# A memory projection whose high and low token parts stand side by side in one 512-column pass

## The chip, the cores and the metric

The kernel runs on one core of one Trainium2 chip, as one launch. The metric is the device time of that launch in microseconds: median 962.98 of 3 runs, 962.02 to 963.68. TensorE (PE in the profile) multiplies, VectorE (DVE) and ScalarE (ACT) do the elementwise work, GpSimd (POOL) helps with some of it, SyncE (SP) issues nearly all transfers.

## The reference

One decoder layer on 512 tokens of width 2048, all in float32. The residual is normed, projected once to the queries, keys, values and gates of three groups of heads (6 block-sparse, 6 forgetting, 4 that attend into 256 memory tokens), each group's output is multiplied by SiLU of its gate, and an output projection, a norm and the residual close it. The part that the change touches is the projection of the memory:

```python
def rms_norm(x, g):
    xf = x.astype(jnp.float32)
    y = xf * lax.rsqrt(jnp.mean(xf * xf, axis=-1, keepdims=True) + EPS)
    return (y * g.astype(jnp.float32)).astype(x.dtype)
...
mkv = jnp.einsum('bmd,de->bme', rms_norm(mem, g_mem[layer]), w_mem_kv[layer])   # (1, 256, 1024)
km, vm = jnp.split(mkv, 2, axis=-1)
out_m = memory_attention(split_heads(qm, N_HEADS_MEM), split_heads(km, N_HEADS_MEM),
                         split_heads(vm, N_HEADS_MEM))
```

## The kernel before, in words

**High and low parts.** Every float32 matrix is split into a rounded high part (type F32R, fp32r in the profile) and the rest, the low part. A product is three passes of TensorE into one PSUM bank: high weight by high token, low weight by high token, high weight by low token. The helper `three` (lines 414 to 418) issues them, one line for each pass, and TensorE loads a 128x128 weight tile before each.

**Strips and pieces.** Weights are taken in strips of 128 output columns. A strip has 16 steps over the inner dimension and comes in two pieces of 8 steps. A piece is loaded by SP into `raw` (four slots); ScalarE writes its high part into `ring` (line 697, `hi`); VectorE (`lo`, `minus`, line 937) or GpSimd (`lo`, line 1279) writes its low part. Which of the two does the first 16 pieces is a list, `POOL_PIECES`: GpSimd has 0 to 5, 7 to 11, 13 and 15; VectorE has 6, 12 and 14. From then on VectorE does all.

**The memory projection.** The first 8 strips (t = 0 to 7) are `w_mem_kv` times the 256 memory tokens: t = 0 to 3 make the keys of the four memory heads, t = 4 to 7 their values. The tokens lie transposed in `memT`, indexed by half (high, low), step and token, with 256 columns for each half and step; so each pass has 256 columns and a bank of 512 is half used. They are multiplied by the gain of the norm but not yet by its reciprocal root. That root, spread over the partitions in `rstd_mem`, comes in where the strip leaves PSUM: line 1125 writes `k_mem`, `copy_v` (line 1012) writes `vT`. Strips alternate between two banks (`strip_ps`), and `strip_free` counts the evictions.

**The order around it.** The order of each engine is written out by hand. For each t, VectorE does: the eviction of key strip t - 1 (for t = 1 to 4), the norm factors and the scaling of one tile of x (`scale_tile`, lines 952 to 969; for t = 1 to 4), the low part of the key (line 937, `y<-k_mem,y`), from t = 5 the eviction of value strip t - 1, the low parts of the next strip's pieces where they are its own, and the low parts of transposed tiles of x (line 977). ScalarE does: the high part of the next strip's first piece, the high part of the key (line 833), the high part of the second piece, squares, and high parts of transposed tiles. So within one t, GpSimd can start on the second piece only when the key of strip t - 1 has been evicted by VectorE and copied by ScalarE. TensorE turns tiles of x between the two halves of strips 3 to 6 (line 454), and turns an evicted value strip back after the next strip (`turn_v`, line 464). Behind the eighth strip come 32 passes for the forget gate (line 575), and then the long run of strips of `w_in` over 512 tokens.

Of the kernel before, what the change touches and what calls it, by code (L numbers as in the profile page):

```python
# [29 lines left out]
F32 = mybir.dt.float32  # L30
F32R = mybir.dt.float32r
BF16 = mybir.dt.bfloat16
ALU = mybir.AluOpType
# [3 lines left out]
P = 128  # L37
D = 2048
S = 512
KT = D // P  # L40
QB = S // P
NMEM = 256
MB = NMEM // P
DH = 128
NA, NB, NM = 6, 6, 4
# [80 lines left out]
def build(nc, x, mem, w_in, b_forget, w_mem_kv, w_out, g_pre, g_post, g_mem, rel_bias, buckets, out):  # L126
    ctx = ExitStack()
    with ctx:
# [3 lines left out]
        def place(name, shape, dt, at=None):  # L132
            off = base[0] if at is None else at
            t = nc.alloc_sbuf_tensor_at(name, shape, dt, offset=off)
            if at is None:
                base[0] = off + (4 * int(np.prod(shape[1:])) + 31) // 32 * 32
            return t, off

        xT, _ = place("xT", [P, 2, KT, S], F32R)
        y, y_at = place("y", [P, 2, NH, S], F32R)  # L140
        raw, _ = place("raw", [P, RING, PW], F32)
# [8 lines left out]
        vT, vT_at = place("vT", [P, S], F32)  # L150
        ident, _ = place("ident", [P, P], F32)
        mask, _ = place("mask", [P, P], F32)
        bias_low, _ = place("bias_low", [P, 6 * P], F32)
        eps, _ = place("eps", [P, 1], F32)
        gains, _ = place("gains", [P, 2, KT], F32)
        relT, _ = place("relT", [BUCKETS + 1, NA], F32)
# [18 lines left out]
        ones, _ = place("ones", [P, P], F32, at=vT_at + 4 * P)  # L175
        gain_rows, _ = place("gain_rows", [KT, 2, P], F32, at=vT_at + 4 * 2 * P)
        k_mem, _ = place("k_mem", [P, NMEM], F32, at=vT_at + 4 * 2 * P)


        hot, _ = place("hot", [BUCKETS + 1, TABLE], F32, at=y_at + 4 * NAB * S)  # L180
# [31 lines left out]
        def sem(name):  # L212
            return ctx.enter_context(nc.semaphore(name))
# [30 lines left out]
        mem_squared = sem("mem_squared")  # L244
        diag_ready = sem("diag_ready")
        rstd_spread = sem("rstd_spread")
        k_taken = sem("k_taken")
        lo_pool = sem("lo_pool")
        part_done = sem("part_done")
# [163 lines left out]
        def _(pe):  # L413
            def three(dst, lhs, rhs, start, stop):

                pe.matmul(dst, lhs[0], rhs[0], start=start, stop=False, skip_group_check=True)  # L416
                pe.matmul(dst, lhs[1], rhs[0], start=False, stop=False, skip_group_check=True)  # L417
                return pe.matmul(dst, lhs[0], rhs[1], start=False, stop=stop, skip_group_check=True)  # L418

            def strip(t, par, rhs, n, between=None):  # L420

                if not isinstance(t, int) or t >= 2:
                    pe.wait_ge(strip_free, t - 1)
                for half in range(2):
                    by_pool, count = lo_count(2 * t + half)
                    pe.wait_ge(lo_pool if by_pool else lo_done, count)
                    w = ring[:, 2 * par + half].rearrange("p h (k m) -> p h k m", m=P)
                    for k in range(PIECE_KT):
                        kt = PIECE_KT * half + k
                        last = three(strip_ps[par][:, 0:n], (w[:, 0, k], w[:, 1, k]), (rhs[:, 0, kt], rhs[:, 1, kt]),  # L430
                                     kt == 0, kt == KT - 1)
                    last.then_inc(piece_used, 1)
                    if half == 0 and between is not None:
                        between()
# [22 lines left out]

            def turn_v(head_v, strip_v, blocks):

                pe.wait_ge(strip_free, strip_v + 1)  # L460
                if not isinstance(head_v, int) or head_v > 0:
                    pe.wait_ge(v_ready, head_v)
                for b in range(blocks):
                    last = pe.transpose(vt_ps[:, P * b:P * (b + 1)], vT[:, P * b:P * (b + 1)], ident[:])  # L464
                last.then_inc(v_turned, 1)
# [224 lines left out]
        def _(act):  # L690
# [137 lines left out]
            for t in range(STRIPS_MEM):  # L828
                next_strip = (t + 1, (t + 1) % 2, (t + 1) // 2)
                hi_strip(next_strip, 0)  # L830
                if 1 <= t <= NM:
                    act.wait_ge(strip_free, t)
                    act.activation(kmv[:, 4 * (t - 1)], k_mem[:], ACTF.Copy
                                   ).then_inc(k_hi, 1)
                hi_strip(next_strip, 1)
                if t == 0:
                    for half in range(2):
                        act.wait_ge(mem_landed[0][half], 16)
                    squares(0)
                    act.wait_ge(mem_squared, 1)  # L840
                    root(1, 0, MB)
                if t >= 6:
                    hi_v(t - 6, kmv[:, 4 * (t - 6) + 2], NMEM)
                if t in TURN_DURING:
                    pair, half = TURN_DURING[t]
                    hi_tiles(pair, 4 * half, 4 * half + 4)
                if t in SQUARE_DURING:
                    squares(SQUARE_DURING[t])
                    root(SQUARE_DURING[t], SQUARE_DURING[t])
                if t == 5:  # L850
                    act.wait_ge(forget_landed, 32)
                    act.wait_ge(wf_cleared, 1)
                    act.activation(wf[:, 0:KT * 64].rearrange("p (k c) -> p k c", c=64)[:, :, 0:NB], wf_raw[:],
                                   ACTF.Copy).then_inc(wf_hi, 1)
# [71 lines left out]
        def _(dve):  # L926
# [77 lines left out]
            def lo_k(head):  # L1004
                dve.wait_ge(k_hi, NM + head.a + 1)
                minus(kv[:, S:2 * S], strip_ps[1][:], kv[:, 0:S]).then_inc(strip_free, 1)

            def copy_v(strip_v, par):

                dve.wait_ge(piece_used, 2 * strip_v + 2)  # L1010
                if isinstance(strip_v, int) and strip_v < STRIPS_MEM:
                    dve.tensor_tensor(vT[:, 0:NMEM], strip_ps[par][:, 0:NMEM], rstd_mem[:], ALU.mult
                                      ).then_inc(strip_free, 1)
                else:
                    dve.tensor_copy(vT[:], strip_ps[par][:]).then_inc(strip_free, 1)

# [99 lines left out]
            for t in range(STRIPS_MEM):  # L1116
                if t == 1:
                    dve.wait_ge(rstd_spread, 1)

                    chain(dve.tensor_copy(rstd_mem[:], o_ps[:, 0:NMEM]))  # L1120
                if 1 <= t <= NM:
                    dve.wait_ge(piece_used, 2 * t)
                    if t > 1:
                        dve.wait_ge(k_taken, t - 1)
                    dve.tensor_tensor(k_mem[:], strip_ps[(t - 1) % 2][:, 0:NMEM], rstd_mem[:], ALU.mult
                                      ).then_inc(strip_free, 1)
                if t in SCALE_DURING:
                    scale_tile(SCALE_DURING[t])
                if 1 <= t <= NM:
                    dve.wait_ge(k_hi, t)  # L1130
                    minus(kmv[:, 4 * (t - 1) + 1], k_mem[:], kmv[:, 4 * (t - 1)]).then_inc(k_taken, 1)
                if t > NM:
                    if t > NM + 1:
                        dve.wait_ge(v_turned, t - 1 - NM)
                    copy_v(t - 1, (t - 1) % 2)
                for half in range(2):
                    lo_strip((t + 1, (t + 1) % 2, (t + 1) // 2), half)
                if t == STRIPS_MEM // 2 + 1:
                    for i, (bank, lo_, hi_) in enumerate(table_banks):
                        dve.wait_ge(table_made, i + 1)  # L1140
                        dve.tensor_copy(table[:, lo_:hi_], bank[0:NA, 0:hi_ - lo_]).then_inc(table_copied, 1)
                if t >= 6:
                    lo_v(t - 6, kmv[:, 4 * (t - 6) + 3], kmv[:, 4 * (t - 6) + 2], NMEM)
                if t == 0:
                    for half in range(2):
                        dve.wait_ge(mem_landed[1][half], 16)
                    dve.tensor_tensor_reduce(waste_mem[:], stage[:, 1], stage[:, 1], 1.0, 0.0, ALU.mult, ALU.add,
                                             sq[:, 1:2]).then_inc(mem_squared, 1)
                    dve.wait_ge(mem_squared, 1)
                    dve.wait_ge(squares_done, 1)  # L1150
                    rstd(1, 0, n=MB)
                    for i in range(MB):
                        dve.tensor_scalar(rstd_diag[:, i], ident[:], stat[:, 4, i:i + 1], None, ALU.mult
                                          ).then_inc(diag_ready, 1)
                if t in TURN_DURING:
                    lo_tiles(*TURN_DURING[t])
                if t == 5:
                    dve.memset(wf[:].bitcast(F32), 0.0).then_inc(wf_cleared, 1)
                    dve.wait_ge(wf_hi, 1)
                    wf_v = wf[:, 0:KT * 64].rearrange("p (k c) -> p k c", c=64)  # L1160
                    minus(wf_v[:, :, 32:32 + NB], wf_raw[:], wf_v[:, :, 0:NB]).then_inc(wf_ready, 1)
# [182 lines left out]
```

## Time and profile before

| what | value |
|---|---|
| median of 3 runs | 962.98 us (962.02 to 963.68) |
| profiled execution, first to last instruction (its span) | 961.3 us |
| median less span | 1.7 us |
| TensorE busy | 940.1 us, 98% of the span, 4556 passes |
| VectorE, ScalarE, GpSimd busy | 405.0, 312.0 and 93.1 us |
| mean granted clock of TensorE | 0.994 of full speed |
| the 384 passes of the memory projection, lines 416 to 418, 128x256 | 38.4, 37.2 and 37.2 us |

The profiled execution's own time has no figure apart from its span; the 1.7 us between span and median stand for launch and end around it. A group's busy time is the time from the start to the modelled end of its instructions; passes of TensorE overlap, so what one of them costs is the distance from its start to the start of the next. Idle time of an engine is put down to the instruction that released it.

### The profile page before, as it was taken

The numbers are of one execution on the slowest core, as the hardware profiler recorded it, in microseconds if no ns is written. First come the engines' busy times: TensorE is split into PE (matmuls) and PEld (weight loads), VectorE is DVE, ScalarE is ACT, GpSimd is POOL, SyncE is SP. The second block draws the span as 40 slices with busy tenths as digits, with TensorE's granted clock in tenths as the row PEclk, the third lists the DMA queues.
The fourth block names the chain that finished last, engine by engine and source line by source line (L and its number), as shares of the span: only waits on it lengthen the run. The fifth ranks groups of instructions, "written<-read, shape, count | busy, mean of one in ns | idle before, by whom it ended". The sixth has DMA issues, their size and how long they took to land.

```text
span 961.3 us, 12115 instructions
## 1 busy us (share of the span) xinstructions
PE 940.1 (98%) x4556; PEld 790.4 (82%) x4556; DVE 405.0 (42%) x724; ACT 312.0 (32%) x546; POOL 93.1 (10%) x84
## 2 busy tenths in 40 slices
PE   7799999999999999999999999999999999999996
PEld 5798888888888888888888888888888888888885
DVE  5884365444333333334343434343434254241424
ACT  6572333323232222223232323232323243242411
POOL 5542057000000000000010101010101000000000
PEclk9899999999999999999999999999999999999999
DMA  9934333343333333333333333333333127341216
GB/s 309 263 93 125 94 114 85 90 105 93 86 97 87 89 97 87 98 87 99 87 98 88 98 87 98 87 98 87 95 80 95 58 88 289 105 125 50 87 36 227
DMA packets 150943, 104.86 MB, mean 109 GB/s; under 512 B 5561, under 2 KB 136665, under 8 KB 149766
## 3 DMA queue, kind: packets, MB, share of 16 engines
q1 hardware_dynamic: 150630, 103.48, 38.5%
q10 hardware_dynamic: 288, 1.05, 0.3%
q8 instruction: 16, 0.26, 0.1%
q14 instruction: 9, 0.07, 0.0%
HBM read 100.29 MB, written 5.79 MB: 110 GB/s over the span
## 4 chain that ended last, share of the span: by engine, by line
PE 95%; DVE 2%; ACT 1%; DMA 1%; issue 0%; SPq 0%; DVEq 0%; ACTq 0%
PE strip_ps L416 25%; PE strip_ps L418 25%; PE strip_ps L417 25%; PE score_ps L416 3%; PE score_ps L418 3%; PE score_ps L417 3%; PE o_ps L520 3%; PE pt_ps L501 2%; PE score_ps L481 1%; PE score_ps L480 1%; PE score_ps L482 1%; PE o_ps L575 1%; PE vt_ps L464 1%; DMA stage<-in_mem_dram 1%; ACT y L736 1%; DVE y L937 1%
## 5 line engine op out<-in xcount | busy, mean ns | idle before, releaser
L416 PE MATMUL strip_ps<-xT,ring 128*128 128x512 f32 x896 | 352.0, 393 | 0.0
L418 PE MATMUL strip_ps<-xT,ring 128*128 128x512 f32 x896 | 349.3, 390 | 0.0
L417 PE MATMUL strip_ps<-xT,ring 128*128 128x512 f32 x896 | 348.9, 389 | 0.0
L418 PEld LDWEIGHTS strip_ps<-xT,ring 128*128 128x128 f32 x896 | 168.2, 188 | 35.6
L417 PEld LDWEIGHTS strip_ps<-xT,ring 128*128 128x128 f32 x896 | 168.4, 188 | 33.4
L416 PEld LDWEIGHTS strip_ps<-xT,ring 128*128 128x128 f32 x896 | 168.2, 188 | 33.3
L697 ACT ACTIVATE ring<-raw 128x1024 fp32r<-128x1024 f32 x128 | 135.1, 1058 | 34.3 <-PE strip_ps L418 34.3
L937 DVE TENSOR_TENSOR ring<-raw,ring 128x1024 fp32r<-128x1024 f32 x115 | 141.0, 1226 | 6.4 <-ACT ring L697 6.3
L1041 DVE MEMSET pace<- 128x1 f32 x36 | 2.1, 59 | 138.8 <-PE score_ps L482 138.8
L1313 POOL TENSOR_TENSOR bias<-bias,mask 128x128 f32<-128x128 f32 x6 | 6.6, 1097 | 553.0 <-DMA bias<-negc_dram 553.0
L937 DVE TENSOR_TENSOR xT<-raw,xT 128x1024 fp32r<-128x1024 f32 x32 | 39.0, 1224 | 41.9 <-ACT xT L697 41.6
L1001 DVE SCALAR_TENSOR_TENSOR q<-strip_ps,q 128x512 fp32r<-128x512 f32 x16 | 11.1, 692 | 102.6 <-ACT q L753 102.6
L753 ACT ACTIVATE q<-strip_ps 128x512 fp32r<-128x512 f32 x16 | 9.6, 598 | 127.9 <-PE strip_ps L418 127.9
L416 PE MATMUL strip_ps<-xT,y 128*128 128x512 f32 x128 | 50.0, 391 | 0.0
L418 PE MATMUL strip_ps<-xT,y 128*128 128x512 f32 x128 | 49.8, 389 | 0.0
L417 PE MATMUL strip_ps<-xT,y 128*128 128x512 f32 x128 | 49.8, 389 | 0.0
L416 PE MATMUL score_ps<-xT,y 128*128 128x512 f32 x128 | 49.8, 389 | 0.0
L417 PE MATMUL score_ps<-xT,y 128*128 128x512 f32 x128 | 49.8, 389 | 0.0
L418 PE MATMUL score_ps<-xT,y 128*128 128x512 f32 x128 | 49.8, 389 | 0.0
L775 ACT ACTIVATE prob<-prob,negmax 128x128 f32<-128x128 f32 (+3 forms) x48 | 27.0, 563 | 67.1 <-DVE negmax L1046 66.7
L697 ACT ACTIVATE xT<-raw 128x1024 fp32r<-128x1024 f32 x32 | 33.7, 1059 | 43.9 <-PE score_ps L418 33.1
L416 PE MATMUL strip_ps<-y,ring 128*128 128x256 f32 x128 | 38.4, 300 | 6.2 <-DVE ring L937 3.3
(164 smaller groups left out, 1021.9 us busy)
## 6 DMA issues: line engine op xcount, KB each, us to landing
raw<-in_w_in_dram SPq DMA_DIRECT2D x112, 512.0 KB, 4.1
raw<-in_w_out_dram SPq DMA_DIRECT2D x32, 512.0 KB, 4.0
raw<-in_w_mem_kv_dram SPq DMA_DIRECT2D x16, 512.0 KB, 6.2
stage<-in_x_dram SPq DMA_DIRECT2D x4, 1024.0 KB, 7.6
xres<-in_x_dram SPq DMA_DIRECT2D x4, 1024.0 KB, 7.5
out_dram<-o_sb SPq DMA_DIRECT2D x16, 256.0 KB, 3.5
toep_dram<-table_dram SPq DMA_DIRECT2D x1, 1536.0 KB
bias<-toep_dram SPq DMA_DIRECT2D x6, 256.0 KB, 2.6
```

The costliest lines, as they stand in the source:

```text
L416: pe.matmul(dst, lhs[0], rhs[0], start=start, stop=False, skip_group_check=True)
L417: pe.matmul(dst, lhs[1], rhs[0], start=False, stop=False, skip_group_check=True)
L418: return pe.matmul(dst, lhs[0], rhs[1], start=False, stop=stop, skip_group_check=True)
L464: last = pe.transpose(vt_ps[:, P * b:P * (b + 1)], vT[:, P * b:P * (b + 1)], ident[:])
L480: pe.matmul(dst[:, 0:n], qs[0], kv[:, 0:n], start=True, stop=False, skip_group_check=True)
L481: pe.matmul(dst[:, 0:n], qs[1], kv[:, 0:n], start=False, stop=False, skip_group_check=True)
L501: last = pe.transpose(pt_ps[g % 2][:, P * i:P * (i + 1)], src, ident[:])
L520: last = pe.matmul(o_ps[:, first:S], v, pT[:, hl_p, kb, first:S], start=(hl_v, hl_p, kb) == (0, 0, 0), stop=(hl_p == 1 and kb == nb - 1), ...
L697: act.activation(dst[:, 0], raw[:, slot], ACTF.Copy).then_inc(hi_done, 1)
L775: last = act.activation(prob[:, i % 2, 0:n], prob[:, i % 2, 0:n], ACTF.Exp, scale=-1.0, bias=negmax[:, i:i + 1], accum_out=rowsum[:, i:i + 1])
L937: return dve.tensor_tensor(dst, a_, hi_.bitcast(F32), ALU.subtract)
L1001: dve.scalar_tensor_tensor(out=q[:, 1], in0=strip_ps[0][:], scalar=SCALE, in1=q[:, 0].bitcast(F32), op0=ALU.mult, op1=ALU.subtract).then_i ...
```

## The change

It is made at four places. In `strip`, where the tokens are the memory's (n is 256), one pass of 512 columns takes the high weight over the high and the low tokens side by side, `rhs[:, :, kt]`; its results stand in the two halves of the bank. A second pass of 256 columns puts low weight by high token on the right half. So a step has two passes in place of three, of 768 columns together as before. In the evictions, `scale_halves` multiplies both halves by `rstd_mem` into `halves` (one instruction of 512 elements, over the place of `bias_low`, which is first written much later) and then waits for itself; a second instruction adds the halves. `strip_free` now counts the multiplication. ScalarE's copy of the key and TensorE's turn of the value wait for two new semaphores that count the addition.

```diff
@@ build
-        bias_low, _ = place("bias_low", [P, 6 * P], F32)
+        bias_low, bias_low_at = place("bias_low", [P, 6 * P], F32)
...
+        halves, _ = place("halves", [P, 2, NMEM], F32, at=bias_low_at)
...
+        k_scaled = sem("k_scaled")
+        v_scaled = sem("v_scaled")
@@ strip (TensorE)
                         kt = PIECE_KT * half + k
+                        if n == NMEM:
+
+                            pe.matmul(strip_ps[par][:, 0:2 * n], w[:, 0, k], rhs[:, :, kt], start=kt == 0, stop=False,
+                                      skip_group_check=True)
+                            last = pe.matmul(strip_ps[par][:, n:2 * n], w[:, 1, k], rhs[:, 0, kt], start=False,
+                                             stop=kt == KT - 1, skip_group_check=True)
+                            continue
                         last = three(strip_ps[par][:, 0:n], (w[:, 0, k], w[:, 1, k]), (rhs[:, 0, kt], rhs[:, 1, kt]),
                                      kt == 0, kt == KT - 1)
@@ turn_v (TensorE)
-                pe.wait_ge(strip_free, strip_v + 1)
+                if isinstance(head_v, int) and head_v < NM:
+                    pe.wait_ge(v_scaled, head_v + 1)
+                else:
+                    pe.wait_ge(strip_free, strip_v + 1)
@@ the strips of the memory (ScalarE)
                 if 1 <= t <= NM:
-                    act.wait_ge(strip_free, t)
+                    act.wait_ge(k_scaled, t)
@@ (VectorE)
+            def scale_halves(t, par):
+
+                one_row = rstd_mem[:]
+                twice = bass.AP(one_row.tensor, one_row.offset, [one_row.ap[0], [0, 2], [1, NMEM]])
+                dve.tensor_tensor(halves[:], strip_ps[par][:].rearrange("p (h t) -> p h t", h=2), twice, ALU.mult
+                                  ).then_inc(strip_free, 1)
+                dve.wait_ge(strip_free, t + 1)
+
             def copy_v(strip_v, par):
 
                 dve.wait_ge(piece_used, 2 * strip_v + 2)
                 if isinstance(strip_v, int) and strip_v < STRIPS_MEM:
-                    dve.tensor_tensor(vT[:, 0:NMEM], strip_ps[par][:, 0:NMEM], rstd_mem[:], ALU.mult
-                                      ).then_inc(strip_free, 1)
+                    scale_halves(strip_v, par)
+                    dve.tensor_tensor(vT[:, 0:NMEM], halves[:, 0], halves[:, 1], ALU.add).then_inc(v_scaled, 1)
...
-                    dve.tensor_tensor(k_mem[:], strip_ps[(t - 1) % 2][:, 0:NMEM], rstd_mem[:], ALU.mult
-                                      ).then_inc(strip_free, 1)
+                    scale_halves(t - 1, (t - 1) % 2)
+                    dve.tensor_tensor(k_mem[:], halves[:, 0], halves[:, 1], ALU.add).then_inc(k_scaled, 1)
```

## Rows read from the trace of the kernel before

**Rows 1.** The page, busy time by engine: us (share of the span) xinstructions.

```profile
PE 940.1 (98%) x4556; PEld 790.4 (82%) x4556; DVE 405.0 (42%) x724; ACT 312.0 (32%) x546; POOL 93.1 (10%) x84
```

**Rows 2.** What TensorE waited for, 0 to 200 us: in total, times, longest.

```profile
PE strip_ps L416 <- DVE ring L937: 3.3, 1, 3.3
PE strip_ps L416 <- POOL ring L1279: 2.8, 3, 1.2
PE o_ps L549 <- DVE rstd_diag L1153: 2.5, 1, 2.5
```

**Rows 3.** The chain that ended last, 24 to 48 us: start, length, work.

```profile
28.14 0.43 DVE rstd_mem L1120
28.59 0.42 DVE k_mem L1125
...
31.11 2.56 DVE y L937
...
33.77 0.42 DVE k_mem L1125
...
36.28 2.50 DVE y L937
...
40.06 0.55 PE strip_ps L416
```

**Rows 4.** VectorE in order of time: start, length, line, operation, output<-inputs.

```profile
28.93 0.14 DVE L952 TENSOR_SCALAR stat<-sq 128x1 f32<-128x1 f32 x1
...
38.70 1.21 DVE L937 TENSOR_TENSOR ring<-raw,ring 128x1024 fp32r<-128x1024 f32 x1
39.84 0.41 DVE L1125 TENSOR_TENSOR k_mem<-strip_ps,rstd_mem 128x256 f32<-128x256 f32 x1
...
45.74 0.42 DVE L937 TENSOR_TENSOR y<-k_mem,y 128x256 fp32r<-128x256 f32 x1
...
59.41 0.42 DVE L1012 TENSOR_TENSOR vT<-strip_ps,rstd_mem 128x256 f32<-128x256 f32 x1
...
99.88 0.69 DVE L1001 SCALAR_TENSOR_TENSOR q<-strip_ps,q 128x512 fp32r<-128x512 f32 x1 [7.16 <-ACT q L753]
```

**Rows 5.** GpSimd in order of time, 30 to 45 us.

```profile
30.50 2.88 POOL L1279 TENSOR_TENSOR ring<-raw,ring 128x1024 fp32r<-128x1024 f32 x1 [4.09 <-ACT ring L697]
35.67 2.82 POOL L1279 TENSOR_TENSOR ring<-raw,ring 128x1024 fp32r<-128x1024 f32 x1 [2.30 <-ACT ring L697]
38.84 5.65 POOL L1279 TENSOR_TENSOR ring<-raw,ring 128x1024 fp32r<-128x1024 f32 x2 [0.34 <-ACT ring L697]
```

**Rows 6.** ScalarE in order of time, 29 to 39 us.

```profile
29.05 0.42 ACT L833 ACTIVATE y<-k_mem 128x256 fp32r<-128x256 f32 x1 [5.37 <-DVE k_mem L1125]
...
37.72 1.04 ACT L697 ACTIVATE ring<-raw 128x1024 fp32r<-128x1024 f32 x1
```

**Rows 7.** TensorE in order of time: passes of 256 and of 512 columns.

```profile
56.26 0.36 PE L416 MATMUL strip_ps<-y,ring 128*128 128x256 f32 x1
...
66.70 0.38 PE L464 MATMUL vt_ps<-ident,vT 128*128 128x128 f32 x2
...
78.96 0.28 PE L416 MATMUL strip_ps<-y,ring 128*128 128x256 f32 x1
...
80.04 0.28 PE L416 MATMUL strip_ps<-y,ring 128*128 128x256 f32 x1
...
300.27 0.39 PE L418 MATMUL strip_ps<-xT,ring 128*128 128x512 f32 x1
...
307.75 0.39 PE L418 MATMUL strip_ps<-xT,ring 128*128 128x512 f32 x1
```

**Rows 8.** Busy time by stretch: PE, PEld, DVE, ACT, POOL, granted clock, DMA share, GB/s.

```profile
24.00:39.30 15.30, 10.25 (x82) 9.79 (x80) 13.95 (x24) 9.01 (x12) 8.58 (x5) 1.00 0.93 274
39.40:46.10 6.70, 6.04 (x28) 6.07 (x29) 6.56 (x9) 1.36 (x2) 5.08 (x2) 0.50 0.84 229
46.20:48.00 1.80, 1.80 (x18) 1.80 (x17) 0.74 (x2) 1.62 (x5) 0.00 (x0) 1.00 1.20 295
```

## The prediction

> **What bounds the kernel now.** I read the page first. TensorE is busy for 940.1 of 961.3 us; VectorE, the next, for 405.0 [rows 1]. So a time changes only where TensorE's own passes change or where it stands idle. Next the list of what TensorE waited for. Up to 200 us it has three entries that bear on the memory projection: 3.3 us for a low part by VectorE, 2.8 us in three waits for low parts by GpSimd, 2.5 us for the norm factors [rows 2]. Asked for from 48 us on, the same view lists nothing. So from there every us that TensorE starts earlier or later, and every us that its passes take less, goes into the end one to one.
>
> The third view, the chain of waits around the longest gap, says who sets it. It runs on VectorE from 28.14 to 39.91 us (38.70 + 1.21): root copied, key strip 0 evicted, norm factors and scaling of a tile, low part of the key, key strip 1 evicted, the same again, and last the low part of piece 6, for which TensorE starts strip 3 at 40.06 [rows 3, 4]. The two evictions in that chain are the ones that the change makes longer. The fourth view, granted clock by stretch, shows a price of the gap: the clock is 1.00 up to 39.3 us, 0.50 from 39.4 to 46.1, and 1.00 again from 46.2 [rows 8]: the two levels, 2.4 and 1.2 GHz, with some 6.8 us at the lower one, 6.1 of them work. The gap of 2.5 us before the spreading of the norm factors [rows 2] lies in the stretch at 1.00 and lowered nothing.
>
> **What the passes save.** A step of the projection has three passes of 256 columns and gets one of 512 and one of 256. By the time from start to start, 9 passes of 256 take 80.04 - 78.96 = 1.08 us, 120 ns each [rows 7]. 33 passes of 512 (11 steps of 3 between the two rows) take 307.75 - 300.27 = 7.48 us, 227 ns each [rows 7]. So two narrow passes, 240 ns, become one wide pass of 227: 13 ns a step. What goes is a fixed cost of a pass and not columns. No row shows a wide pass over two separate runs of tokens. Its bounds: 0 ns saved, if it costs what its two halves cost apart; and 39 ns, if the step cost nothing beyond its 768 columns at 2.4 GHz (320 ns against 360). I take 13, since the 512-column row is the same kind of pass with the same type and the same load of weights.
>
> The saving counts only where TensorE does not wait afterwards. Strips 0 to 2 end in the waits above, so there it makes the gap wider and nothing else. The first half of strip 3 runs at half clock; I give it nothing (at most 8 steps, 0.1 us). The second half of strip 3 and strips 4 to 7 are 8 + 64 = 72 steps: 72 x 13 ns = 0.94 us saved (0 to 2.8).
>
> The Trainium skill speaks against this term: TensorE: Matmul & The Clock Gate, Back-to-back issue gap, gives N/2.4 + 2.5 ns between warm passes. By that rule, an estimate, a step would save one fixed cost of 2.5 ns, 0.18 us in all, and the change would come out 0.8 us worse than by the rows. The trace does not agree with its fixed cost: 256 columns at 2.4 GHz are 107 ns and the row has 120.
>
> **What the evictions add.** The old one takes 0.42 us and the next VectorE instruction starts 0.34 us after it (28.59 to 28.93) [rows 3, 4]; ScalarE's copy of the key starts at 29.05, 0.46 us after it [rows 6]. The new one has two parts. The multiplication reads 512 elements from PSUM; the nearest row of that size takes 0.69 us [rows 4]. Waiting for itself costs little: the copy before the eviction ends at 28.57 and the eviction, which waits for it, starts at 28.59 [rows 3]. The addition reads 256 elements twice from SBUF; the same form on the key takes 0.42 us where GpSimd is idle [rows 4]. So the old 0.42 becomes 0.69 + 0.02 + 0.42 = 1.13, and both the next instruction of VectorE and ScalarE's copy come 0.71 us later. Bounds of that: 0.60 if the broadcast row comes free, and 0.42 + 2.5 more where GpSimd is in the way.
>
> GpSimd can be. The low part of the key, 256 elements that take 0.42 us alone, takes 2.56 and 2.50 us in the chain, and ends 0.3 and 0.3 us behind GpSimd's subtractions, which run from 30.50 to 33.38 and from 35.67 to 38.49 [rows 3, 5]. (The Trainium skill, SBUF — State Buffer, Who interferes with whom: an instruction of VectorE with two SBUF inputs and one of GpSimd that reads SBUF exclude each other, the first to start going first. The trace agrees.) The eviction itself reads PSUM and one SBUF tile and is not held up. The addition is of the other sort. For t = 1 it falls at 28.59 + 0.71 = 29.30; GpSimd is idle until 30.50, and its next piece waits for ScalarE, which waits for this key [rows 5, 6]. For t = 2 the eviction moves from 33.77 to 34.48, the addition to 35.2; GpSimd's piece ends by 33.38 + 0.71 = 34.1, and the next again waits for this key. So both additions are clear, by about 1 us. GpSimd, ScalarE and VectorE all move by the same 0.71 each time, and so does what they do to each other. **The chain of the gap grows by 2 x 0.71 = 1.42 us**, and strip 3 starts at 41.48 instead of 40.06.
>
> The other six evictions. For t = 3 the multiplication starts at 39.84 + 1.42 = 41.26, the addition at 41.97; there GpSimd has piece 8 until 38.84 + 1.42 + 2.83 = 43.1, so the addition ends near 43.4, over 1 us late [rows 4, 5]. Behind it stand ScalarE's copy, the high part and low part of piece 9, and VectorE's scaling and low key. Piece 9 is then done at about 47.7, and TensorE needs it for the second half of strip 4, at 56.26 before [rows 7]: hidden by 10 us. The slot of piece 9 also comes free some 3 us later for SP's load of piece 13, needed well behind that. t = 4 has no chain to TensorE that is close. The value strips: the first is evicted at 59.41 and turned by TensorE at 66.70 [rows 4, 7], 7 us for 0.7. The next strips' pieces (12, 14) lie behind these evictions on VectorE and are needed one strip later, each over 4 us off. `strip_free` comes 0.27 us later and guards a bank that TensorE wants one strip later. These cost nothing while the distances stand; gone, each would cost 0.71.
>
> **Sum.** +1.42 (gap) - 0.94 (72 steps) = +0.48 us against the profiled span of 961.3, so 961.8. The median of the runs lies 1.7 us above the span, which I carry over: 962.98 + 0.48 = **963.5**. This assumes that as much work falls into half clock as before. It has a small side: if all 6.8 us of half clock now met work, where 0.7 met the gap, +0.35, 963.8. With the bounds of the pass (0 to 2.8) the case itself runs from 961.6 to 964.8.
>
> **Rivals.**
> *The half clock ends when it ended.* If it returns near 46.15 whatever TensorE has done, strip 3's later start loses only half as much: 1.42 us of half-rate work is 0.71 of full-rate work. Then 0.71 - 0.94 = -0.23, 962.8. For it: no start or end of TensorE's work marks 46.15. Against: nothing in one trace separates this from a length that counts from the start.
>
> *The clock does not fall.* Piece 5 now comes 0.71 us later, at 34.1, and strip 2 can't start its second half before; its 8 steps of 0.347 us then end near 36.9, after a stop inside the strip, and the gap is some 4.5 us long. Before, 6.1 us of work (40.06 to 46.15) ran at half rate, 3.05 lost. If the new split of work and idle time escapes the lower level, 0.48 - 3.05 - 0.1 = -2.7, 960.3. For it: a 2.5 us gap escaped. Against: the large gap grows.
>
> *GpSimd gets in ahead of piece 6 (the other side).* VectorE begins piece 6 at 38.70 and GpSimd piece 8 at 38.84 [rows 4, 5]: 0.14 us decide. Both move by 1.42 by my sum; ScalarE's high part (37.72 + 1.04) sets GpSimd, and GpSimd's own piece 7 sets VectorE. If VectorE comes 0.15 us later against it, piece 6 waits for piece 8, 2.83 us, and strip 3 with it: 0.48 + 2.83 = +3.3, 966.3.
>
> *The wide pass costs its columns only* (39 ns a step): 1.42 - 2.8 = -1.4, 961.6. The row of 227 ns for 213 ns of columns speaks against it. That passes do not fall from 384 to 256 is not to be expected; the code is unconditional there.
>
> **How the numbers follow.** Forecast 0.40; half clock ends in its place 0.20; clock does not fall 0.13; GpSimd first 0.12; columns only 0.05; an addition or another stall that I placed wrongly, +1 to +3 us, 0.10, six of these ten past the line. A measurement of this kernel can tell 0.2%, 1.9 us, from no change. Faster: 0.13. Slower: 0.12 + 0.06 = 0.18. Same: 0.69. The range takes in all but the collision and the worst stalls: 960.2 to 965.5; the forecast's own is 961.6 to 964.8.
>
> **What would show it.** 128 passes fewer, 4428. Strips 4 to 7 with 347 ns a step. k_mem's first addition near 29.3 and 0.42 us long, the one at t = 3 over 1 us long. Strip 3 starting at 41.5 with the last wait for piece 6. The granted clock tells the first two rivals from the forecast, and the order of pieces 6 and 8 the third. A wait of TensorE behind 50 us, or additions of 2 us in the gap's chain, would make it wrong.

## The result, and the profile after

| | runs | median, us | range |
|---|---|---|---|
| before | 19 | 962.80 | 962.02 to 963.87 |
| the change | 19 | 964.26 | 962.98 to 966.16 |

The ratio is 1.0016, with a 95% interval of 1.0009 to 1.0023: slower by 1.5 us (0.16%), and less than the 0.2% that I took for the limit of what can be told. A second measurement, in another session, gave 1.0018 (1.0009 to 1.0027). Forecast was 963.5, "same" at 0.69. The forecast direction (+0.48) is right and its size a third of what came. The rest of this document is about the missing 1.0 us: what of it the runs explain, and what they leave open.

The page of the profiled execution: 128 passes fewer, TensorE no less busy, VectorE 7 us busier.

```profile
span 962.8 us, 11867 instructions
...
PE 940.5 (98%) x4428; PEld 783.9 (81%) x4428; DVE 411.8 (43%) x732; ACT 311.6 (32%) x546; POOL 94.4 (10%) x84
```

What TensorE waited for, up to 200 us, as [rows 2]. The wait for piece 6 grew from 3.3 to 4.2 us; nothing is listed behind it.

```profile
PE strip_ps L436 <- DVE ring L951: 4.2, 1, 4.2
PE strip_ps L436 <- POOL ring L1301: 2.7, 3, 1.3
PE o_ps L563 <- DVE rstd_diag L1175: 2.6, 1, 2.6
```

The chain around the gap, as [rows 3] (start, length, work).

```profile
29.53 0.44 DVE rstd_mem L1142
29.99 0.70 DVE halves L1026
30.71 0.42 DVE k_mem L1148
...
33.23 2.55 DVE y L951
...
35.88 0.70 DVE halves L1026
36.61 0.42 DVE k_mem L1148
...
39.12 2.49 DVE y L951
41.61 1.15 DVE ring L951
42.75 0.14 issue
42.89 0.77 PE strip_ps L436
```

The absolute times mislead here. This execution copied the root at 29.53 where the other did at 28.14 [rows 3]: the first load of memory tokens, which the change doesn't touch, was the start of both chains and took 7.38 us against 5.98. A second profile of the change copied it at 28.05. So read distances from the copy. From there to strip 3 it is 42.89 - 29.53 = 13.36 us; before, 40.06 - 28.14 = 11.92. That is +1.44, for two evictions of 0.70 + 0.03 + 0.42 in place of 0.42. At the other end, the 32 passes for the forget gate (line 575 before, 589 after) are a good end mark, because from their start to the end of the span it is 880.8 us in both kernels (961.3 - 80.54; 962.8 - 82.00):

```profile
81.87 0.38 PE L478 MATMUL vt_ps<-ident,vT 128*128 128x128 f32 x2
82.00 0.48 PE L589 MATMUL o_ps<-xT,wf 128*128 128x512 f32 x1
```

From the copy to that mark: before 80.54 - 28.14 = 52.40 us, after 52.47. By the two profiled executions, the change costs 0.1 us once the start is taken out. The medians say 1.5. One pair of profiles did not show what the change does on average.

The clock is the first hint (stretches as in [rows 8]):

```profile
30.00:41.00 11.00, 8.14 (x46) 6.64 (x44) 10.55 (x18) 8.41 (x12) 5.36 (x2) 1.00 0.89 314
41.10:47.80 6.70, 4.91 (x15) 4.27 (x16) 6.53 (x11) 1.86 (x3) 4.59 (x3) 0.50 0.65 175
47.90:60.00 12.10, 12.10 (x79) 10.07 (x78) 11.93 (x22) 10.02 (x22) 6.73 (x3) 1.00 0.31 87
```

Half clock lasted about as long as before (6.8 us), but began earlier against the work: strip 3 began at 42.89 and met 4.9 us of it, not 6.04 [rows 8]. By the start of strip 3 and the end of the half clock it is 5.0 against 6.1, and half of the difference, 0.56 us, was given back. So this pair went as my first rival said: +1.44 - 0.56 - 0.83 (the passes, below) = +0.05, where 0.07 was read.

VectorE, in order of time, at the key of strip 2 (t = 3). The addition is held until GpSimd is done, as forecast, at 1.88 us for 0.42:

```profile
41.53 1.21 DVE L951 TENSOR_TENSOR ring<-raw,ring 128x1024 fp32r<-128x1024 f32 x1
42.67 0.68 DVE L1026 TENSOR_TENSOR halves<-strip_ps,rstd_mem 128x512 f32<-128x512 f32 x1
43.38 1.88 DVE L1148 TENSOR_TENSOR k_mem<-halves 128x256 f32<-128x256 f32 x1
```

And GpSimd (start, length), which began piece 8 at 41.67, 0.14 us behind VectorE's piece 6, the same distance as in [rows 4, 5]:

```profile
41.67 3.30 POOL L1301 TENSOR_TENSOR ring<-raw,ring 128x1024 fp32r<-128x1024 f32 x1 [0.35 <-ACT ring L711]
```

### The profile page after: what moved, and what is told of

The parts are those of the page before. It is cut to its first block, busy times and chain, and to the rows that moved or that the text cites. A ratio compares the mean times of both kernels' runs of the same rounds, so it can differ in the third digit from the quotient of the medians.

```text
span 962.8 us, 11867 instructions
## 1 busy us (share of the span) xinstructions
PE 940.5 (98%) x4428; PEld 783.9 (81%) x4428; DVE 411.8 (43%) x732; ACT 311.6 (32%) x546; POOL 94.4 (10%) x84
## 4 chain that ended last, share of the span: by engine, by line
PE 95%; DVE 2%; ACT 1%; DMA 1%; issue 0%; SPq 0%; DVEq 0%; ACTq 0%
PE strip_ps L420 24%; PE strip_ps L422 24%; PE strip_ps L421 24%; PE score_ps L422 3%; PE score_ps L421 3%; PE score_ps L420 3%; PE o_ps L534 3%; PE strip_ps L436 2%; PE pt_ps L515 2%; PE strip_ps L438 1%; PE score_ps L495 1%; PE score_ps L494 1%; PE score_ps L496 1%; DMA stage<-in_mem_dram 1%; PE o_ps L589 1%; PE vt_ps L478 1%
## 5 line engine op out<-in xcount | busy, mean ns | idle before, releaser
L951 DVE TENSOR_TENSOR ring<-raw,ring 128x1024 fp32r<-128x1024 f32 x115 | 143.1, 1245 | 6.1 <-ACT ring L711 6.0
L436 PE MATMUL strip_ps<-y,ring 128*128 128x512 f32 x128 | 48.5, 418 | 7.0 <-DVE ring L951 4.2
```

Source lines behind the costliest of these rows:

```text
L436: pe.matmul(strip_ps[par][:, 0:2 * n], w[:, 0, k], rhs[:, :, kt], start=kt == 0, stop=False, skip_group_check=True)
L951: return dve.tensor_tensor(dst, a_, hi_.bitcast(F32), ALU.subtract)
```

## The experiments

Every kernel ran in 9 to 11 timed executions, beside 31 to 33 of the kernel before on the same chip in each of three sessions (medians of before: 962.37, 962.38, 962.46). "Mean clock" is the mean granted clock over all executions of a kernel; 0.001 of it is 1.9 us at half clock. Before has 0.9938, 0.9943 and 0.9939; the change has 0.9918 (19 executions, the first result) and 0.9925 (11, the second measurement, beside the 0.9943). It is a weak witness. All 14 profiles also show 3.6 to 6.6 us of half clock at the very end, where TensorE has no work left, and four of them (the change, evictions only, two strips old, before with 6 fillers) show 3.4 us between 8 and 14 us. So two executions can differ by 0.002 and more without any difference behind the gap.

The theories that the expectations name: **A**, my sum as it stands (passes -0.94, evictions +1.42, half clock alike). **B**, A and a longer gap that on average puts more work at half clock. **C**, the changed program delays the start of the memory stage. **D** came later: with the clock up, VectorE becomes the slower engine behind the gap.

### Each half of the change alone

**Passes only.** The new passes are put into the kernel before, with the old eviction.

```diff
+                        if n == NMEM:
+                            pe.matmul(strip_ps[par][:, 0:2 * n], w[:, 0, k], rhs[:, :, kt], start=kt == 0, stop=False, ...)
+                            last = pe.matmul(strip_ps[par][:, n:2 * n], w[:, 1, k], rhs[:, 0, kt], start=False, ...)
+                            continue
```

> The 512-column pass and the 256-column pass of the change, with the old eviction, which reads the left half of the bank only: the product of the low weights and the low tokens' part are left out of k and v. The chain of the gap is as before. Theory A (my sum: passes -0.94 us, evictions +1.42 us, half clock as before): 0.8 to 1.0 us faster than before, strip 3 starts as far behind the copy of the root as before (11.9 us). Theory B (A, and a longer gap puts more work into half clock on average): the same here, since the gap grows by only 0.1 to 0.2 us. Theory C (the passes or the changed program delay the start of the memory stage, 28.14 to 29.53 us in the two profiles): slower than before or no faster, with the root copied near 29.5 us in the profile.

Measured: 961.30 us, ratio 0.9990 (0.9981 to 0.9999), -1.1 us by the medians. From copy to strip 3 it is 40.32 - 28.40 = 11.92, exactly the old gap. Theories A and B stand. The new passes do not delay the copy of the root: it came at 28.40.

**Evictions only.** The old passes, with the two-part eviction on the left half twice.

```diff
-                dve.tensor_tensor(halves[:], strip_ps[par][:].rearrange("p (h t) -> p h t", h=2), twice, ALU.mult
+                left = strip_ps[par][:, 0:NMEM]
+                left2 = bass.AP(left.tensor, left.offset, [left.ap[0], [0, 2], [1, NMEM]])
+                dve.tensor_tensor(halves[:], left2, twice, ALU.mult
...
-                    dve.tensor_tensor(k_mem[:], halves[:, 0], halves[:, 1], ALU.add).then_inc(k_scaled, 1)
+                    dve.tensor_tensor(k_mem[:], halves[:, 0], halves[:, 1], ALU.max).then_inc(k_scaled, 1)
```

> The three old passes, with the two-part eviction: the multiplication reads the left half twice, and a maximum of the two equal halves stands in for the addition, so the result is whole. Theory A: +1.4 us against before, strip 3 starts 13.3 to 13.4 us behind the copy of the root. Theory B: +1.4 plus up to 1 us, since the gap is as long as that of the change less 0.1 us. Theory C: +1.4, or no more than A if the passes are the cause.

Measured: 964.75 us, 1.0025 (1.0015 to 1.0035), +2.4 us. The chain grew by what was forecast (42.97 - 29.59 = 13.38 from copy to strip 3, +1.46), so the evictions cost about 0.9 us more than the chain shows. The two halves add up to the whole (-1.1 + 2.4 = +1.3). The missing us is on the side of the evictions, and not in the passes. B had room for it, A had not. Two things in this run speak against taking that for a proof of B. The mean clock is 0.9932 beside 0.9938, so hardly lower. And its profile copied the root at 29.59, late like that of the change (29.53).

This leaves theory C open for the evictions. In the 14 profiles of this study the copy lies between 28.05 and 29.59. The six profiles of kernels with the two-part eviction in the chain show 28.05, 28.28, 28.54, 28.88, 29.53 and 29.59, the eight others 28.14 to 28.88. The evictions come behind the copy, and the change has it at 28.05 too, so nothing in the traces says that they move it. But no timed execution shows where its copy was, and a later one on average would go into the time in full.

### The gap filled with other passes

The fillers are passes into a bank that nobody reads then. They are meant to keep TensorE at work until piece 6 is ready; n is 10 for the change, 8 and later 6 for the kernel before.

```diff
                 strip(t, t % 2, memT, NMEM, lambda: between(t))
+                if t == 2:
+                    for _ in range(n):
+                        pe.matmul(o_ps[:, 0:NMEM], ones[:], rstd_diag[:], start=True, stop=True)
```

> The change, with 10 more passes (the form of line 549, 0.35 us each) in the gap before strip 3, into a bank that nobody reads then; they should end before piece 6 is ready. The granted clock should then stay at 1.00 up to strip 7. Against the change: 2.5 us faster (half of the 5.0 us that its profile shows at half clock) in executions like the profiled one. Against the kernel before: A, that loses 3.05 us to half clock: -2.6 us. B: the kernel before loses less than that on average, so -1.5 or less, and the change loses about 1 us more than it.

> The kernel before, with 8 of those passes in its gap. Clock at 1.00 throughout the memory stage. A: 3.0 us faster than before, and the change with its gap filled is +0.4 to +0.6 us against this one while the plain pair differs by +1.46, which then needs B. If the filled pair differs by 1.4 as well, the clock explains none of it and one of my two terms (1.42, 0.94) is wrong.

Measured: the change filled 962.88, 1.0006 (0.9997 to 1.0015); before filled with 8, 961.79, 0.9992 (0.9983 to 1.0001). Both gained less than I expected. For the kernel before there is a plain reason: the fillers ran past the end of the gap. In the profile with 8, the last filler ended at 41.81, piece 6 was ready at 40.50, and strip 3 began 12.77 us behind the copy instead of 11.92. So I ran it with 6:

> The kernel before with 6 of those passes in its gap of 3.3 us. With 8, they ended at 41.8 us in the profile, some 1.1 us behind the moment when piece 6 was ready (40.7), so they gave back part of what the clock gained. With 6 they end in time: 1 to 1.5 us faster than before, and no wait in front of strip 3 longer than 0.8 us.

Measured: 960.95, 0.9988 (0.9979 to 0.9997), -1.4 us, the time that was expected. Its profile does not bear out the way: half clock had struck at 28.7 to 32.1, TensorE was late, and the fillers ended at 41.07, behind piece 6 (40.20); strip 3 began 12.33 us behind the copy, 0.4 late. In a later run with 6 (the control below) they ended at 39.52, in time. This is the fastest kernel of the study; it beats both. So the kernel before loses on average 1.4 us or more to the clock after its gap, and not the 3.05 that its one profile would give (6.1 us of work at half rate).

The change, filled, is 0.51 us above before. Before is 0.58 below with 8 fillers (same chip) and 1.43 below with 6: 1.1 and 1.9 us apart. B said 0.4 to 0.6, so B was not enough. The executions with the highest clock say it most plainly, since they have next to no half clock in the stage: the four of the change, filled, with a clock of 0.997 took 962.20 to 962.57 us, the four of before with 8 fillers and 0.998 took 960.41 to 960.75. That is 1.8 us at full clock, where my sum has 0.48. The trace of the change, filled, has what was missing. Its waits:

```profile
PE strip_ps L436 <- POOL ring L1304: 3.3, 4, 1.3
PE o_ps L563 <- DVE rstd_diag L1178: 2.5, 1, 2.5
...
PE vt_ps L478 <- DVE y L954: 0.9, 1, 0.9
```

The wait in front of strip 3 is gone, and there is a new one, of TensorE for the low part of a value. TensorE in order of time where it stands:

```profile
79.79 0.41 PE L478 MATMUL vt_ps<-ident,vT 128*128 128x128 f32 x2 [0.94 <-DVE y L954]
```

A second hold-up stands in no list of PE's waits, since the weight load waited: in the tile turn of strip 5, for the low part of a transposed tile. That turn took 0.34 us longer than in the change's own profile.

```profile
62.12 0.42 PEld L465 LDWEIGHTS pt_ps<-ident,stage 128*128 128x128 f32 x4 [0.36 <-DVE xT L994]
```

The chain that ended last shows the same. In the change without fillers it leaves VectorE at strip 3 (42.75, above) and stays on TensorE. In the change, filled, it stays on VectorE, but for some 3 us of ScalarE, up to that turn (start, length, work):

```profile
52.46 1.82 DVE k_mem L1151
...
58.92 3.14 DVE xT L994 x8
62.06 0.61 DVE halves L1029
62.70 0.55 DVE vT L1038
...
77.03 1.87 DVE ring L954 x2
78.90 0.32 issue
79.22 0.43 DVE y L954
79.65 0.14 issue
79.79 0.41 PE vt_ps L478 x2
```

With the clock up over the whole stretch, VectorE is what can't follow. Busy time over 54 us of the memory stage (columns as in [rows 8]; VectorE's is the third pair), first of the change filled, then of a kernel with the old evictions and fillers (the control below):

```profile
28.00:82.00 54.00, 52.53 (x313) 44.90 (x312) 51.18 (x89) 33.57 (x62) 22.36 (x8) 1.00 0.62 179
```

```profile
28.00:82.00 54.00, 53.24 (x417) 50.84 (x416) 45.44 (x80) 33.79 (x62) 23.33 (x9) 1.00 0.68 193
```

51.2 of 54 us against 45.4 (the clock is 1.00 in both; the second kernel also has piece 14, 1.2 us, off VectorE). The clock did not bring that load: over the same 54 us VectorE has 44.75 in the profile of before and 50.96 in that of the change, both with 6.8 us of half clock. The change brought it, and the half clock gave VectorE time for it. This is theory D: the passes' saving counts only while TensorE is the slower of the two.

### Is it the six other evictions?

**The change again**, for the same chip as the ones below.

> The change as it is, beside the kernel before on the chip of the three kernels below. Theory A (passes -0.94 us, evictions +1.42 us, clock alike): +0.5 us. Theory B (A, and the longer gap puts about 2 us more per execution of strip 3's work at half clock): +1.3 to +1.6 us, and a mean granted clock about 0.002 lower than that of before in the same job (0.002 x 962 us x 2 = 3.8 us more at half clock, part of it idle).

Measured: 963.63, 1.0018 (1.0009 to 1.0027), mean clock 0.9925 against 0.9943, close to what B said. The copy-to-strip distance was 41.41 - 28.05 = 13.36 again.

**Old for two strips.** Strips 0 and 1 keep the old passes and evictions.

```diff
-                        if n == NMEM:
+                        if n == NMEM and t >= 2:
...
-                    act.wait_ge(k_scaled, t)
+                    if t > 2:
+                        act.wait_ge(k_scaled, t - 2)
+                    else:
+                        act.wait_ge(strip_free, t)
...
-                    scale_halves(t - 1, (t - 1) % 2)
-                    dve.tensor_tensor(k_mem[:], halves[:, 0], halves[:, 1], ALU.add).then_inc(k_scaled, 1)
+                    if t > 2:
+                        scale_halves(t - 1, (t - 1) % 2)
+                        dve.tensor_tensor(k_mem[:], halves[:, 0], halves[:, 1], ALU.add).then_inc(k_scaled, 1)
+                    else:
+                        dve.tensor_tensor(k_mem[:], strip_ps[(t - 1) % 2][:, 0:NMEM], rstd_mem[:], ALU.mult
+                                          ).then_inc(strip_free, 1)
```

> The change for strips 2 to 7, the old passes and the old eviction for strips 0 and 1, whose passes end in a wait anyway and whose evictions are the two in the chain of the gap. A and B alike: the chain is that of before, 72 steps are 12 to 13 ns shorter, so 0.8 to 1.0 us faster than before and 2.3 us faster than the change; mean clock as before. If it is no faster than before, the six other evictions cost something that I hold for hidden.

Measured: 961.94, 0.9995 (0.9986 to 1.0004): -0.4 us by the medians, 1.7 us faster than the change. Removing the two evictions from the chain takes back all of the loss, though 1.7 us is less than the 2.3 expected. Half of the passes' saving seems missing, but the interval holds both 0 and -0.9, so this run alone doesn't settle it.

> The same with 6 more passes (about 0.43 us each, 2.6 us) in the gap before strip 3, which is about 3.6 us long. B: less time at half clock, so 0.5 to 1.5 us faster than the one without, unless VectorE can't follow: with the gap filled the change itself showed a wait of 0.9 us of TensorE for the low part of a value. Then the gain is smaller by as much, and the wait stands in the trace.

Measured: 961.81, 0.9994 (0.9985 to 1.0004). The fillers brought nothing here, where they brought 1.4 us to the kernel before. In its profile they ended at 42.1 us, behind piece 6 again, because half clock had also struck strip 2; and the wait for the low part of a value stands there with 0.3 us.

**Relief for VectorE.** Piece 14 goes to GpSimd, 9 fillers.

```diff
-POOL_PIECES = [0, 1, 2, 3, 4, 5, 7, 8, 9, 10, 11, 13, 15]
+POOL_PIECES = [0, 1, 2, 3, 4, 5, 7, 8, 9, 10, 11, 13, 14, 15]
```

> The change with 9 fillers in its gap and the low part of piece 14 moved from VectorE to GpSimd. Theory D: with the clock up, the change is bound by VectorE (51.2 of 54 us busy against 44.8 before), and the 0.94 us wait in front of the turn of the third value strip takes back the 0.94 us that the passes save. Moving 1.2 us from VectorE behind strip 5 should remove that wait: about 0.9 us faster than the change filled without it (962.88 us), so about -0.4 us against before, and no wait of TensorE for VectorE near 80 us. If the wait was not what cost, the time stays near 962.9.

Measured: 962.84, 1.0006 (0.9997 to 1.0015): no gain over 962.88. The wait shrank from 0.94 to 0.31, but GpSimd needed 4.96 us for pieces 14 and 15 and a wait for it appeared in front of strip 7:

```profile
74.17 0.47 PE L436 MATMUL strip_ps<-y,ring 128*128 128x512 f32 x1 [0.24 <-POOL ring L1304]
...
80.36 0.41 PE L478 MATMUL vt_ps<-ident,vT 128*128 128x128 f32 x2 [0.31 <-DVE y L954]
```

So the expectation failed, and this run did not prove D by removal. It moved the limit and left the time: from the copy to the passes for the gate it is 51.65 us, as without the move (51.67), and the chain that ended last is on VectorE still.

> The change, not filled, with piece 14 moved to GpSimd. D says: only executions with little half clock meet the limit of VectorE, so 0 to 0.5 us faster than the change. B alone: no difference. In a profile with half clock in the gap no wait of TensorE for VectorE should stand near 80 us in either.

Measured: 963.54, 1.0009 (1.0000 to 1.0018), the same as the change within the intervals. It has one use: its profile caught a short half clock (41.3 to 44.7), and with it copy to gate is 80.29 - 28.54 = 51.75 us.

> Old passes and evictions for strips 0 and 1, the change for strips 2 to 7, 5 fillers, piece 14 on GpSimd. Should collect both gains: -0.9 (passes) and -1.4 (fillers, as in the kernel before with 6 of them): about 960.1 us, 2.3 us faster than before and the fastest of all. If it is no faster than the kernel before with 6 fillers (-1.4), the passes' saving is still lost to VectorE.

Measured: 961.55, 0.9989 (0.9980 to 0.9998), -0.9 us; not the fastest. The passes' saving did not come on top of the fillers'.

> Control: the kernel before with 6 fillers and piece 14 on GpSimd. VectorE had slack there (no wait for it behind strip 3), so the move gives nothing: the same as with 6 fillers alone, -1.2 to -1.6 us against before.

Measured: 961.05, 0.9988 (0.9979 to 0.9997): as with 6 fillers alone (960.95). The control holds.

### The two floors

A floor is here the shortest time that a kernel's stage can take at full clock. The profiles together, as distances in us (copy of the root, start of strip 3, start of the passes for the gate; the last column is the half clock that lies behind the gap, before the gate):

| kernel | copy to strip 3 | strip 3 to gate | copy to gate | half clock |
|---|---|---|---|---|
| before | 11.92 | 40.48 | 52.40 | 6.8 |
| the change | 13.36 | 39.11 | 52.47 | 6.8 |
| the change again | 13.36 | 39.24 | 52.60 | 6.8 |
| evictions only | 13.38 | 40.52 | 53.90 | 6.8 |
| two strips old | 11.93 | 39.76 | 51.69 | 6.8 |
| passes only | 11.92 | 38.39 | 50.31 | 3.4 |
| change, relief | 13.36 | 38.39 | 51.75 | 3.4 |
| before, 6 fillers, relief | 11.94 | 37.74 | 49.68 | 0 |
| change, 10 fillers | 13.37 | 38.30 | 51.67 | 0 |
| change, 9 fillers, relief | 13.39 | 38.26 | 51.65 | 0 |
| two strips old, 5 fillers, relief | 11.93 | 38.30 | 50.23 | 0 |
| two strips old, 6 fillers | 12.88 | 37.45 | 50.32 | 0 |
| before, 6 fillers | 12.33 | 37.84 | 50.16 | 0 |
| before, 8 fillers | 12.77 | 37.86 | 50.64 | 0 |

In the last three rows the fillers ran past piece 6 and made strip 3 late.

Where the full 6.8 us of half clock follow the gap, the change and the kernel before are within 0.1 to 0.2 us of each other, and each single edit does about what the sum says (evictions +1.50, passes in strips 2 to 7 -0.71 for -0.94). Where the clock stays up, the kernel before falls by 2.7 us, to 49.68. The change falls by 0.8 to 0.9 and then stands at 51.67: behind strip 3 it needs 38.30 where the old passes need 37.74, because its evictions hold TensorE up. Passes only, with the old evictions, needs 38.39 with 3.4 us of half clock, by an estimate 36.7 without its 1.7 of loss: 1.0 less than the old passes. The two floors are 2.0 us apart. The old evictions in strips 0 and 1 take the floor down from 51.67 to 50.23, by what the chain lost.

The timed runs show the floors too. Of 97 executions of before in the three sessions, 16 lie at 960.36 to 961.02, apart from the rest (the 19 of the first result begin at 962.02); of 30 of the change none is below 962.68.

That is one part of the missing us: before can be quicker than its profile by up to 2.7 us, the change by 0.8 or 0.9. It is not all. With the copy at 28.1, 52.4 or 52.5 to the gate, 880.8 behind it and 1.8 around the span, the two profiles make 963.1 for before and 963.2 for the change. The medians of before were 962.80 and 962.38, so 0.3 and 0.7 below. Those of the change were 964.26 and 963.63, so 1.1 and 0.4 above. The change is also often slower than its profiles with an early copy: by a later copy, or by more half clock than 6.8 us. A timed execution doesn't show which.

## Why the prediction was right or wrong

**What bounds it: right for the kernel before.** TensorE in the end, one to one. From the gate's passes on, all kernels need the same 880.8 us. The change, at full clock, is bound by VectorE up to the gate.

**The passes: right in size.** By the distances between TensorE's turns in the two profiles, 8 steps of strip 5 with their turn went from 4.61 to 4.52 us and the 16 of strip 7 from 5.98 to 5.78, 11 to 12 ns a step. Two neighbours show the step:

```profile
74.02 0.39 PE L436 MATMUL strip_ps<-y,ring 128*128 128x512 f32 x1
74.25 0.27 PE L438 MATMUL strip_ps<-y,ring 128*128 128x256 f32 x1
74.36 0.40 PE L436 MATMUL strip_ps<-y,ring 128*128 128x512 f32 x1
```

0.34 to 0.35 us a step for 0.360; forecast 0.347. Two runs of tokens in one pass cost no more than one. Summed behind the half clock, the stretch from the tile turns of strip 3 to the gate took 0.83 us less (82.00 - 48.04 = 33.96, and 80.54 - 45.32 = 35.22 before, less 0.43 of half clock in the latter), 0.94 was forecast. The passes alone gave -1.1 us in the timed runs. (The 2.5 ns of fixed cost a pass that the Trainium skill states, TensorE: Matmul & The Clock Gate, Back-to-back issue gap, would have given 0.2 us, an estimate; the page gives it for isolated passes, and here the measurement decides against it.)

**The evictions in the chain: right, to 0.04 us.** 1.42 forecast, 1.44 in both profiles of the change and 1.46 with evictions alone. Without these two evictions the loss is gone, so they are its cause. The addition at t = 3 was held up as said, and both in the chain were clear of GpSimd.

**The six other evictions: wrong.** "These cost nothing while the distances stand" was read from a trace in which TensorE lost 3 us to its clock and so arrived late everywhere. The 7 and 4 us of distance were partly that loss: the first value strip has 7.3 us from its eviction to its turn in the profile of before, and 4.8 in the control at full clock. With the clock up, VectorE is busy for 95% of the stretch and TensorE waits for it: 0.94 us listed, and 1.1 us by the distance from one turn to the next (6.89 for 5.78), with 0.34 more in strip 5. I named the slack and did not ask how much of it the half clock lent. I also held each eviction against it by itself, where the delays add up on VectorE: the eviction of the third value strip begins 44.75 us behind the copy in the control and 47.61 in the change, filled. And I let only the addition at t = 3 meet GpSimd; in the change, filled, the one at t = 4 does too, 1.82 us for 0.42.

**The sum: short by 1.0 us.** "This assumes that as much work falls into half clock as before." It took one execution with the full 6.8 us of half clock for all. The profile of before has 6.1 us of work at half rate, worth 3.05, but filling the gap gained 1.4 on average; and the change, with the longer gap, has a mean clock 0.002 lower. So the term that was mis-sized is the difference in half clock, set to zero, together with the limit of VectorE, priced at nothing, that keeps the change from profiting when the clock stays up: what came is +1.0 us. How the 1.0 is shared between these two and a later copy of the root is not settled, since a timed execution shows its mean clock but not where it fell. That the answer "same" held is partly luck: +1.5 us is clear of no change, and 0.4 us more would have crossed my line of 1.9.

**The rivals.** The half clock ending in its place fits both profiles of the change (6.8 us long again, some 0.5 us given back), at 0.2 chance; as a forecast of the medians, 962.8, it is further off than mine. The clock did not stay up in any profile of the change without fillers. GpSimd did not get ahead of piece 6: 0.14 us before, 0.14 and 0.13 after. Columns only: no. Another stall, +1 to +3 us, at 0.10: the median's +1.5 lies there, but neither profile of the change has a wait of TensorE behind strip 3; only the filled ones have.

## What to carry to other kernels

Before a saving on the bounding engine is booked, ask whether the trace shows it at its full clock: slack that other engines have behind a slow stretch is partly lent by that stretch. Add up the delays along an engine before holding them against the slack. A fused pass that moves work to the evictions should be kept out of the strips whose eviction lies on a chain to the next wait. And where timed executions differ by more than the effect, one profile of each kernel is a sample: compare distances between fixed marks, and make a kernel in which the varying part can't happen.

## What the hardware showed that I had not expected

At 1.2 GHz a pass has no fixed cost: in the change's strip 3 a step of 512 + 256 columns takes 44.95 - 44.31 = 0.64 us, which is 768 columns at that clock. A step of three passes takes as long there (before, 41.48 - 40.84 = 0.64), so the change saves nothing. The 13 ns a pass exist only at 2.4 GHz.

```profile
44.31 0.63 PE L436 MATMUL strip_ps<-y,ring 128*128 128x512 f32 x1
44.73 0.41 PE L438 MATMUL strip_ps<-y,ring 128*128 128x256 f32 x1
44.95 0.63 PE L436 MATMUL strip_ps<-y,ring 128*128 128x512 f32 x1
```

Much the same gap doesn't have the same effect twice. Behind 11.92 us from copy to strip 3, half clock lasted 6.8 us in one profile and 3.4 in another (passes only); and in six of the profiles it also struck between 27 and 34 us, behind a gap of 2.5 us that lowered nothing in the kernel before [rows 2, 8]. Half clock in itself says little of the time: with 6 fillers, executions of before with a mean clock of 0.998 took 960.67 to 960.85 us, and those with 0.993 and 0.994 took 961.09 and 961.14. Passes for nothing in a gap can pay: six of them, 2.75 us long, made the kernel 0.12% faster.
